# A one-layer decoder step on one core: item 0's rows from the ranks, router and experts in one block, and the distance term moved from TensorE to VectorE

## The reference, cut to what matters

```python
proj = h @ w_in                                  # q, k, v for 8 stick-breaking heads and 4 differential heads
# stick-breaking: A[t,s] = sigmoid(z_ts) * prod_{s<j<t} (1 - sigmoid(z_tj)), s < t
# differential:   z = q.k * scale - slope_h * (q_pos - k_pos);  p = softmax(z);  a = p1 - lam * p2
x = layer_norm(alpha * x + concat(sb_out, rms_norm(d_out)) @ w_out)
# router: top 4 of 32 experts, softmax over the four; each expert: clamped SwiGLU, 1024 -> 2048 -> 1024
y = layer_norm(alpha * x + sum_e gate_e * expert_e(x))
```

## Time and profile before

| | us |
|---|---|
| runs shown | 1315.05, 1315.53, 1315.60 (median 1315.53) |
| profiled execution, its own time | 1318.82 |
| its span, first to last instruction | 1316.9 |
| TensorE busy | 1269.1 (96%) |
| VectorE, ScalarE, GpSimd busy | 457.0, 261.5, 85.3 |
| block 1; block 2; block 3 | 0 to 293.6; 293.6 to 350.3; 350.3 to 1316.9 |

### The profile page before, as it was taken

The page is one execution under the profiler, slowest core; times in us unless marked ns, Lnnn a source line. Parts: engine busy times, 40 slices in busy tenths (PEclk is TensorE's granted clock), DMA queues, the critical chain, the costliest instruction groups (busy, mean ns, idle before and its releaser), DMA issues.

```text
span 1316.9 us, 19565 instructions
## 1 busy us (share of the span) xinstructions
PE 1269.1 (96%) x7690; PEld 515.0 (39%) x7691; DVE 457.0 (35%) x983; ACT 261.5 (20%) x606; POOL 85.3 (6%) x92
## 2 busy tenths in 40 slices
PE   7999999999999999999999999999999999999995
PEld 6355446654433333333333333333333333333331
DVE  0265457866723322223322222332222332222225
ACT  1243348742511101001101000110100110100002
POOL 2023235300020000000000000000000000000000
PEclk9999999999899999999999999999999999999998
DMA  9669889993699999999999995999999999999992
GB/s 353 256 250 373 313 316 381 368 375 113 259 367 407 428 429 426 429 428 429 429 427 428 428 429 232 406 426 429 430 427 429 427 428 429 428 428 427 428 429 87
DMA packets 53308, 498.38 MB, mean 378 GB/s; under 512 B 6793, under 2 KB 7945, under 8 KB 26386
## 3 DMA queue, kind: packets, MB, share of 16 engines
q1 hardware_dynamic: 41746, 430.68, 78.3%
q0 software_dynamic: 11520, 67.11, 13.1%
HBM read 493.58 MB, written 3.93 MB: 378 GB/s over the span
## 4 chain that ended last, share of the span: by engine, by line
PE 47%; DMA 23%; ACT 2%; issue 1%; DVE 0%; SPq 0%; ACTq 0%; DVEq 0%
PE psum L2096 25%; DMA arena<-in_w_gate_up 23%; PE psum L2143 11%; PE psum L1462 4%; PE psum L2077 3%; PE psum L1477 2%; PE psum L1470 1%; ACT arena L2173 1%; ACT arena L2192 1%; DVE arena L2338 0%; PE psum L2044 0%; PE psum L2063 0%; DVE arena L2313 0%; ACT L2209 0%; ACT arena L2203 0%
## 5 line engine op out<-in xcount | busy, mean ns | idle before, releaser
L2096 PE MATMUL psum<-arena 128*64 128x512 f32 x2112 | 462.2, 593 | 11.8 <-DMA arena<-in_w_gate_up 11.2
L2096 PEld LDWEIGHTS psum<-arena 128*64 128x64 f32 x2112 | 150.9, 137 | 316.0 <-issue 287.7
L2143 PE MATMUL psum<-arena 128*64 128x512 f32 x1056 | 233.9, 595 | 3.3
L2281 DVE TENSOR_SCALAR arena<-psum 128x512 f32<-128x512 f32 x33 | 22.8, 692 | 613.2 <-PE psum L2096 613.2
L2143 PEld LDWEIGHTS psum<-arena 128*64 128x64 f32 x1056 | 72.9, 137 | 150.2 <-issue 131.9
L2234 DVE SCALAR_TENSOR_TENSOR arena<-psum,arena 128x1024 f32<-128x1024 f32 (+1 forms) x96 | 103.3, 1103 | 69.4 <-PE psum L2081 37.2
L2188 ACT ACTIVATE arena<-arena 128x512 f32<-128x512 f32 x33 | 20.8, 630 | 455.6 <-DVE arena L2281 455.6
L1462 PE MATMUL psum<-arena 128*64 128x512 f32 x408 | 93.4, 592 | 0.0
L1192 DVE STREAM_TRANSPOSE arena<-arena 128x1024 f32<-128x1024 f32 x64 | 75.2, 1218 | 2.2 <-DVE arena L1292 1.1
L2077 PE MATMUL psum<-arena 64*128 64x512 f32 x264 | 65.9, 615 | 2.3 <-issue 2.3
L2196 ACT ACTIVATE arena<-psum 128x512 f32<-128x512 f32 x33 | 19.7, 597 | 239.8 <-PE psum L2143 239.8
(11 more groups left out here) (265 smaller groups left out, 1006.0 us busy)
## 6 DMA issues: line engine op xcount, KB each, us to landing
arena<-in_w_gate_up SPq DMA_DIRECT2D x128, 2048.0 KB, 19.5
arena<-in_w_down SPq DMA_DIRECT2D x62, 2048.0 KB, 16.5
arena<-in_w_in SPq DMA_DIRECT2D x12, 1024.0 KB, 11.5
arena<-in_w_out SPq DMA_DIRECT2D x4, 1024.0 KB, 10.5
arena<-in_w_down SPq DMA_DIRECT2D x4, 1024.0 KB, 8.5
arena<-in_x_prompt SPq DMA_DIRECT2D x4, 512.0 KB, 4.8
out<-arena SPq DMA_DIRECT2D x8, 256.0 KB, 5.5
arena<-in_ln_g SPq DMA_DIRECT2D x2, 512.0 KB, 7.2
```

Source lines behind the costliest of these rows:

```text
L2096: ins = nc.tensor.matmul(psum[64 * h:64 * h + 64, n, :], x_k, slot[k][:, col:col + 512], start=False, stop=(k == KD - 1))
L2143: ins = nc.tensor.matmul(psum[64 * h:64 * h + 64, 7, :], h_k, slot[s][:, col:col + 512], start=(k == 0), stop=(k == KD - 1))
```

## The change: what it does

1. **Start.** ScalarE issues the loads of the identity and the page table, in place of SyncE. The `pick_run` product and its copy come after all three turns of x, and TensorE waits for the copy (`runs_ready`) only where it first writes the bank the product is in.
2. **Differential units.** The identity matmul with `abias` goes; VectorE adds `abias` to the scores of both halves while it reads them from PSUM, writes the sum to `keep` or `left` in SBUF, releases the scores (`z_used`), and takes the maxima of the sum. ScalarE's exponents read the sum. VectorE's order becomes: keys of u+1 half 0, rows of u-2, maxima of u, keys of u+1 half 1, distances, factors. ScalarE takes the piece's sigmoids before the unit's exponents.
3. **Item 0's rows.** Item 0 is expert 0's first 64 tokens, so its places are the ranks of expert 0: `first_rows` multiplies the pick of expert 0 by the rank and compares, one token block at a time. The rest of the tables comes after. The bias matmuls of item 0 move ahead of the last rank.
4. **One block.** Router and experts are one block. Engines that read counts wait for `routed`. Three of the four spares of expert 1 and `b_down` are issued during the router.
5. **Item 0.** The turn of the started-list is after k=3, the tables after k=6, the turn of the gates after the fetch, the `b_down` products after the turn of item 1's rows; the gates' sums, item 1's rows and the weights table are made on VectorE behind item 0's start.

```diff
-                sp.dma_start(page_i, a["page_table"]).then_inc(table_loaded, 16)
-                sp.dma_start(ident, consts[:, 0:P]).then_inc(ident_loaded, 16)
...
+                act.dma_start(ident, consts[:, 0:P]).then_inc(ident_loaded, 16)
+                act.dma_start(page_i, a["page_table"]).then_inc(table_loaded, 16)
...
-                    if y:
-                        nc.tensor.matmul(z_of(u, h), ident, const["abias"], start=True, stop=False)
...
-                    own.link(nc.vector.tensor_reduce(row_max[:, 0:2], psum[:, 2 * (u % 2):2 * (u % 2) + 2, 0:KEYS_Q], AX.X, ALU.max))
+                    z, distance = leaning[u % 2], const["abias"].rearrange("p (o k) -> p o k", o=1).to_broadcast([P, 2, KEYS_Q])
+                    own.link(nc.vector.tensor_tensor(z, psum[:, 2 * (u % 2):2 * (u % 2) + 2, 0:KEYS_Q], distance, ALU.add))
+                    dve.sem_inc(z_used, 1)
+                    own.link(nc.vector.tensor_reduce(row_max[:, 0:2], z, AX.X, ALU.max))
...
-                    exponents(u)
                     if PIECES[p][0] == 0:
                         keep_piece(p)
+                    exponents(u)
...
-                    maxima(u)
-                    store_rows(u - 2)
                     if more:
                         turn_keys(u + 1, 0)
+                    store_rows(u - 2)
+                    maxima(u)
+                    if more:
+                        turn_keys(u + 1, 1)
                     if PIECES[p][0]:
                         distances_of_piece(p)
                     if p:
                         factors(u - 1)
-                    if more:
-                        turn_keys(u + 1, 1)
...
+                def first_rows(n):
+
+                    b = order[n]
+                    nt = BLOCKS[b][1]
+                    rank = psum[0:nt, 3 if n < 2 else 4, n % 2 * EXPERTS:n % 2 * EXPERTS + 1]
+                    link.link(nc.vector.tensor_tensor(slot_in[0:nt, b:b + 1], picked[0:nt, b, 0:1], rank, ALU.mult))
+                    nc.vector.tensor_scalar(pick_rows[:, b, :], const["slot1"][:, 0:SLOTS], slot_in[:, b:b + 1], None,
+                                            ALU.is_equal).then_inc(pick_ready, 1)
...
                 dve.wait_ge(ranked, 3)
+                first_rows(2)
+                off_mean(2, 1)
+                scale(2, 0)
+                link.wait()
+                scale(2, 1)
...
-                rows_of_item(dve, 0)
-                off_mean(2, 1)
-                scale(2, 0)
-                link.wait()
-                scale(2, 1)
...
+                load_spare(2)
+                sp.wait_ge(projected, 5)
                 for s in (8, 10):
-                    sp.wait_ge(projected, 5)
                     load_weights(sp, 0, s)
+                load_spare(0)
+                sp.wait_ge(rows_ready, 6)
+                load_spare(1)
...
-                        if k == 5 and first:
-                            tables()
-                        if k == 6 and first:
-                            turn_gates()
+                        if k == 3 and first:
+                            list_items()
+                        if k == 6 and first:
+                            tables()
                     fetch(t + 1)
                     if first:
-                        pe.wait_ge(b_down_loaded, 32)
-                        pe.wait_ge(weight_copied, 2)
-                        down_bias(0, PART[0])
-                        pe.wait_ge(table_done, 2)
-                        down_bias(1, PART[1])
+                        turn_gates()
...
                     turn(t + 1)
                     if first:
-                        pe.wait_ge(base_ready, 1)
+                        pe.wait_ge(b_down_loaded, 32)
+                        pe.wait_ge(weight_copied, 2)
+                        down_bias(0, PART[0])
+                        pe.wait_ge(table_done, 2)
+                        down_bias(1, PART[1])
```

More of the change, by code:

```diff
@@ L1497, in mark_expert @@
                                            number, None, ALU.is_equal).then_inc(expert_marked, 1)
+        top[0] = item_end
+        gate_in, up_in, sig, hid, hidT, y_rows = (room(512) for _ in range(6))
+        b_down, weightT = room(512), room(TOKENS)
+        base = room(3 * D).rearrange("p (b d) -> p b d", b=3)
+        scatter = room(TOKENS)
+        item_gate = room(3 * TABLE_ITEMS).rearrange("p (b i) -> p b i", b=3)
+        gate_tmp = room(TOP_K * TABLE_ITEMS).rearrange("p (k i) -> p k i", k=TOP_K)
@@ new lines, in decoder_step @@
+        y_out = sem("y_out")
+        last_cols = room(16)
+        halves, minus_mean, variance, roots = last_cols[:, 0:6], last_cols[:, 6:9], last_cols[:, 9:12], last_cols[:, 12:15]
+        pair = room(P)
+        ln_halves = room(D).rearrange("p (n d) -> p n d", n=2)
+        off = room(D, at=top[0])
+        spare.append(room(SLOT))
+        assert top[0] <= tables_at
+        spare.append(room(SLOT, at=tables_at))
+        last_order = (0, 1, 2)
+        mean_set = (4, 6, 7)
+        PART = ((5, 6), (3, 4), (5, 6))
@@ L1637, in _, with turn, fetch, tables @@
                 keep_warm(1)
+                pe.sem_inc(combined, SEED)
+                def turn(t):
+                    pe.wait_ge(xg_ready, t + 1)
+                    turn_rows()
+                def fetch(t):
+                    pe.wait_ge(pick_ready, 3 * t + 3)
+                    for b in range(3):
+                        ins = fetch_block(b, first=(b == 0), last=(b == 2))
+                    ins.then_inc(fetched, 1)
+                def tables():
+                    for n, b in enumerate(order):
+                        nt = BLOCKS[b][1]
+                        pe.wait_ge(slot_done, 8 * n + 8)
+                        pe.wait_ge(places_set, n + 4)
+                        for k in range(TOP_K):
+                            ins = nc.tensor.matmul(psum[:, 3, 0:TABLE_ITEMS], slot_hot[0:nt, b, k, :], item_hot[0:nt, b, k, :],
+                                                   start=(n == 0 and k == 0), stop=(n == 2 and k == TOP_K - 1))
+                    ins.then_inc(table_done, 1)
@@ new lines, in _ @@
+                extras = items(pe, body, routed)
+                pe.wait_ge(drained, 3 * extras + (3 * EXPERTS + SEED - 3))
+                pe.wait_ge(scatter_ready, extras + EXPERTS)
+                pe.wait_ge(xg_copied, extras + (EXPERTS + 1))
+                pe.wait_ge(y_copied, extras + EXPERTS)
+                for b in (0, 2, 1):
+                    scatter_rows(b, LAST_PART[b])
+                pe.wait_ge(marks_set, 4)
+                pe.wait_ge(var_ready, 5)
+                nc.tensor.matmul(psum[:, 5, 0:1], pair, halves[:, 4:5], start=True, stop=True).then_inc(sums_done, 1)
@@ new lines, in _, with body @@
+                for c in range(2):
+                    nc.scalar.activation(weightT[EXPERTS * c:EXPERTS * c + EXPERTS, :], psum[0:EXPERTS, 4, 0:TOKENS], ACT.Copy
+                                         ).then_inc(weight_copied, 1)
+                def body(t, first=False):
+                    act.wait_ge(gate_clamped, t + 1)
+                    nc.scalar.activation(sig, gate_in, ACT.Sigmoid, scale=SIG_ALPHA).then_inc(sig_ready, 1)
+                    copy_rows(t + 1)
+                    copy_x(t + 1)
+                    act.wait_ge(hid_turned, t + 1)
+                    nc.scalar.activation(hidT, psum[:, 7, :], ACT.Copy).then_inc(hid_copied, 1)
+                    act.wait_ge(w_used[RING - 2], t + 1)
+                    if not first:
+                        act.wait_ge(combined, 3 * t + SEED)
+                    nc.scalar.activation(y_rows, psum[:, 7, :], ACT.Copy).then_inc(y_copied, 1)
@@ L2267, in _ @@
                 dve.sem_inc(weight_ready, 1)
+                for c in range(2):
+                    nc.vector.tensor_tensor(pair[:, 64 * c:64 * c + 64], ident[:, 0:64], ident[:, 64:128], ALU.add
+                                            ).then_inc(marks_set, 1)
+                dve.sem_inc(drained, SEED)
                 def body(t, first=False):
```

560 lines of the change are left out of this document (248 added, 312 removed).

## The result

The change made the kernel slower: 1332.76 us median (1327.17 to 1334.02, 4 runs) against 1315.57 (4 runs), ratio 1.0117, 95% interval [1.0099, 1.0135]. The forecast was 1309.8 with a range of 1305.0 to 1315.5. On another chip the same two kernels gave 1327.93 and 1316.84, ratio 1.0091 [1.0076, 1.0107]. Executions of the changed kernel differ among themselves by more (7 us) than those of the kernel before (2 to 4 us).

The account below looks back on a forecast made before the run. TensorE, busy 1269.1 of 1316.9 us, was taken as the bound, so other engines count only where it waits. Start -2.3, units -0.4, router -6.3, item 0 +3.2 gave -5.7 unrounded: 1309.8 from 1315.53, range 1305.0 to 1315.5.

Parts of the forecast that it names:

- the start: Kernel start up to the first projection: earlier loads and turns of x save 2.3 us, bounds 0.9 to 4.0.
- the loop through ScalarE: Differential units: ScalarE's sigmoids, tables and exponents make an 11.5 us loop against 11.33, so units 9 to 13 cost +1.0.
- the wait of 2.4 in item 0: Item 0: TensorE idles 2.4 us ahead of the turn of item 1's rows.
- the router: Router up to item 0: item 0 starts at 344.0 in place of 350.29, -6.3 us, bounds -4 to -8.5.
- the shift of item 1 is the shift of the end: Item loop: all behind item 1's start at 382.44 moves with it, so its shift is the change's whole gain.
- unit 8: Differential unit 8: the wait of 1.81 and its half clock go, half 1's keys come about 0.8 late: -2.7 us.
- rival (a): Eight new waits in units 9 to 15 and item 0 drop the clock, 1.7 us a fall; six or more falls 0.07, one to five 0.2.
- the exponents' 1.54: ScalarE's loop in the differential units: the unit's exponents were put at 1.54 us of the 11.5.
- Rival (e): ScalarE's table switches: a drain of 1.38 more each would add 13.8 + 1.4 us, giving 1325.0; chance under 0.01.
- unit 14 at 0: Unit 14: the 1.47 wait goes, one of some 3.4 comes, less the 1.08 and the loop's slack: no net change.
- unit 15 at +1.3: Unit 15: maxima stand uncovered behind the rows of u-2 (about 0.6) and VectorE's new sum (0.70): +1.3 us.
- Item 0 at +3.2: Item 0: its new order and waits for ScalarE lengthen it from 25.06 to 28.3 us up to hid's copy: +3.2.

Follow-up runs that it names:

- a0: The change itself, unaltered, run on a second chip: 1327.93 us against 1316.84 for the kernel before there, ratio 1.0091.
- a1: The change with its differential units (maxima, exponents, identity matmul, all three orders) as in the kernel before: 1336.17 us against 1335.36 before on its chip, ratio 1.0002.
- c1: The change with both the differential units as before and item 0's gates copied later by ScalarE: 1311.10 us against 1316.84 before, ratio 0.9951.
- a4: The change with ScalarE copying item 0's turned gates behind the sigmoid and the copy of item 1's rows: 1341.32 us against 1335.36 before, ratio 1.0035.
- d2: The kernel before plus five ScalarE copies ahead of unit 15's exponents, to stall TensorE about 2 us: 1324.00 us against 1316.84 before, ratio 1.0044.
- b1: The kernel before with only the change's start part: 1331.82 us against 1334.22 before on its chip, ratio 0.9982.
- b2: The kernel before with only VectorE's sum in place of the identity matmul, all orders kept: 1336.45 us against 1334.22 before, ratio 1.0015.
- e1: The change with exponents before sigmoids, VectorE's factors before second key turn (unit 15: maxima before rows), item 0's gates copied later: 1328.97 us against 1334.22 before, ratio 0.9961.
- a2: The change with ScalarE taking the unit's exponents ahead of the piece's sigmoids again: 1341.08 us against 1335.36 before on its chip, ratio 1.0035.
- a3: The change plus two unread filler matmuls ahead of each unit's second scores and two ahead of its weights' turn: 1348.57 us against 1335.36 before, ratio 1.0094.
- d1: The change with VectorE's factors ahead of the piece's distances and, in unit 15, maxima ahead of rows: 1319.39 us against 1316.84 before, ratio 1.0032.
- e4: d1 plus item 0's gates copied later and one unread filler matmul at each of two places a unit: 1329.86 us against 1334.22 before, ratio 0.9963.

## Why the prediction was wrong

**Right**, each to half a microsecond or so: the start (-2.5 for -2.3, and alone -2.4); the price of VectorE's sum (708 ns for 700); that the loop through ScalarE would bind and that TensorE would wait ahead of the second scores; the wait of 2.4 in item 0; the router, -6.2 in a0, where no half clock fell into it (50.48), but -5.0 in the first profile, with 3.4 us at half, and -3.4 in a1 and c1, with the same 6.8 as before; and that the shift of item 1 is the shift of the end, to 1.4.

**Right by luck: unit 8**, -2.8 for -2.7. The waits shrank by 0.4 and not by 1.0, the identity matmuls, which its sum left out, gave 1.1, and the stretch at half clock stands behind the border, in unit 9, and is 6.8 long in place of 3.4. In a0's profile, with the same wait of 1.44, it is not there.

**Wrong: the clock.** The sum has no term for the clock behind the new waits; it stands in rival (a) alone, and there the price of a fall was wrong, and with it its chance. The rival named the mechanism and every place (units 9 to 15, item 0), and it was given 0.07. Its price, 1.7 a fall, was read off one row, 3.3 us at half in 190.7 to 194.0. The stretches measured in units 9 to 15 and item 0 are 3.4 to 20.5 us long (one of 30.7 in a4 lies on the stalls of unit 9), most of them 7 or more: the first profile has five with 41 us in all. So it takes no six falls to make the change slower: two of 10 to 14 us, at half of that each, are more than the 5.8 forecast. The trace of before held a warning that I passed over: the stretch behind the wait of 1.34 was 6.8 us long (337.4 to 344.2), twice the one I took the price from.

The second half of the same error is the question asked. I compared single waits with those of 1.81, 1.34 and 1.47, and held waits under 1.81 for harmless. In the change two waits of about 1.0 and 0.8 stand 2 us apart in every unit from 10 to 13 that runs at full clock, and the clock fell behind those of unit 10 in the first profile and of units 10 and 12 in a0's, but not behind those of units 12 and 13 in the first. d2's single wait of 1.90 did not bring it down in the profiled execution nor, by their granted clocks, in four others of twelve. Why executions of one kernel differ in this isn't settled by these runs.

**Wrong: the exponents' 1.54.** They were taken from rows that read PSUM, while the change makes them read SBUF: 743 ns in place of 474. The loop was 12.0, not 11.5: 2.5 over units 9 to 13. Rival (e), a drain at each switch of tables, is out: the exponent starts 0.02 behind its table load (236.13 + 1.28, and 237.43).

**Wrong: unit 14 at 0 and unit 15 at +1.3.** The waits came near to what was worked out (3.10 and 2.09 for 3.4 and 1.4); what followed them did not: 13.7 us at half clock in the end of block 1. Over the profiles that end is 25.3 with no half clock (a1, b1, b2, c1, e1), 27.7 with 5.7 us of it in the tail (a0), 28.1 with 7.5 (a2), 33.1 with 13.7 (the change, a3, a4) and 34.6 with 20.5 (d1): about half the stretch, plus the wait.

**Item 0 at +3.2** was 35.4 in place of the measured 37.8, and 34.4 is what is left when half of its 6.8 us at half clock is taken off. So the term was 1.0 too high without the clock and 2.4 too low with it.

Put together: of the 22.6 us lost in the profiled execution, the waits and the longer loop make 8.8 (units 9 to 13 at 12.0 in place of 56.1 in all, 4.0; unit 14, 1.4; the end of the block less half of its 13.7 at half clock, 1.0; item 0 less half of its 6.8, 2.4), and the other 13.8 go with the clock. By that sum the change without new stretches at half clock would have been some 5 faster than before in its profile. Of these, 3.7 lie in the two stages that the change does not touch (the 2.3 and the 1.4 above), so its own part would be some 1.5, well short of the forecast's 5.8: the longer loop (4.0 lost for 1.0) and unit 14 (1.4 for 0) are most of the gap. No run shows this by itself; e4, which has the fillers but also the mended orders, stands at -4.4. The 13.8 are of the profiled execution, and not of the 17.2 between the medians.

## What to carry to other kernels

A wait that is put on TensorE is not priced by its length. Here waits of 0.8 to 3.1 us were followed in some executions by nothing and in others by 3 to 20 us at half clock, so a change that takes work off TensorE and lets it wait for ScalarE or VectorE instead can lose several times what it saves. Give each new wait a price and a chance of its own in the sum, and take the price from the longest stretch that the trace shows, not from the first; even that (6.8) was too low here, where 10 to 14 came. And look at the granted clock of every execution, not only at the profiled one.

When a change has parts, the ones that shorten a chain which nothing else covers (the start, item 0's rows from the ranks) keep their gain; here they were worth 5.7 us once the rest was undone. And where an order of work is changed on an engine with tables, a copy that waits for TensorE belongs behind the function whose table can be loaded in the idle time: moving it saved 2.0 us, and 3.4 to 5.1 of half clock.

## What the runs showed of the hardware that I had not expected

- ScalarE's exponent with a column as bias and a running sum takes 743 ns for 256 columns read from SBUF and 474 read from PSUM, with the same rearranged order of the columns (steps of 32 columns); for 8 columns it is 288 and 265. So the difference grows with the columns. It isn't the memory alone: in the same trace, by the groups of instructions of the whole span, the exponents of the pieces, with a bias and a sum too, read 256 columns of SBUF in order and take 499:

```profile
L1075 ACT ACTIVATE arena<-arena 128x256 f32<-128x256 f32 x8 | 4.0, 499 | 2.0 <-DVE arena L1325 1.9
```

  The Trainium skill, "ScalarE: Activation LUTs", section "What ACT_TABLE_LOAD costs", gives for such an instruction about 280 ns and 0.833 a column, by which an estimate is 493: the trace agrees for PSUM (474) and for SBUF read in order (499), and not for SBUF read in steps of 32 (743). That the step is the only difference isn't shown, since the pieces' exponents also write where they read.
- The granted clock's stretches at half are of very different length (3.4 to 20.5 us) behind waits of similar length, and the same kernel gives executions 7 us apart (d2) or 18 (d1), in groups that their mean granted clocks tell apart (0.992 and 0.987; 0.987 and 0.972). The wait of 1.81 in unit 8 is followed by 3.4 us at half clock in before's profile and by none in c1's and d2's.
- TensorE at half clock is not idle less but busy more: busy share alone (96% before and after) shows nothing of it, the clock line and the length of a repeated group do (2.28 against 3.85 for the same eight matmuls).
